# Sample rows of a down product from whole fp32 operands in two column tiles, and another order of projection groups

## The reference, cut to what matters

```python
# input projection: one product, its columns split into seven groups
z = _rms_norm(x, g_attn) @ w_in                      # (tokens, 1024) @ (1024, 2840)
qa, zc, zs, zw, gl, qb, zb = jnp.split(z, ...)       # q, k parts: RMS norm per head, gain, rotary
...
# channel mixer behind the attention, width 2816
h = _rms_norm(x, g_ffn)
a = h @ w_gate
c = conv_b + sum(conv_w[k] * ext[:, k:k + S] for k in range(3))   # ext: earlier rows, then a
y = x + (jax.nn.silu(c) * (h @ w_up)) @ w_down
```

## Time and profile before

| | |
|---|---|
| median of 3 runs | 2040.55 us (2034.24 to 2045.2) |
| profiled execution | 2043.56 us, of it the span 2041.8 us |
| mean granted TensorE clock | 0.976 |
| busy: PE, DVE, ACT, POOL | 92%, 54%, 40%, 13% of the span |
| projection, first to last product | 39.5 to 336.1 us |
| compression and attention | 340 us to about 1064 us |
| output projection and channel mixer | about 1064 us to the end |

### The profile page before, as it was taken

How to read it: one execution, slowest core, us unless ns; L and a number is a source line. 1 busy time by engine, 2 the same in 40 slices (tenths; PEclk the granted TensorE clock), 3 DMA queues, 4 the chain that set the end, 5 groups by cost and what they waited for, 6 DMA issues and landing times. The chain is left out here.

```text
span 2041.8 us, 30807 instructions
## 1 busy us (share of the span) xinstructions
PE 1884.3 (92%) x11675; PEld 1548.7 (76%) x11675; DVE 1108.5 (54%) x2625; ACT 820.3 (40%) x1739; POOL 273.1 (13%) x347
## 2 busy tenths in 40 slices
PE   5997999989998888888869999999999999999998
PEld 4776776877887777777757878888888887887886
DVE  5866872337776677777754434444444444444444
ACT  4444441117777666666643232212212212212211
POOL 1000000004444344444320000000000000000000
PEclk8998999989999999999989999999999999999999
DMA  5333233415665222222335223023023023024002
GB/s 178 111 115 120 88 114 102 138 41 154 175 169 145 84 88 86 85 87 82 104 90 174 62 62 104 25 79 103 26 78 103 28 76 104 29 75 144 31 11 92
DMA packets 171945, 192.12 MB, mean 94 GB/s; under 512 B 55302, under 2 KB 138502, under 8 KB 169528
## 3 DMA queue, kind: packets, MB, share of 16 engines
q1 hardware_dynamic: 169458, 175.56, 27.6%
q0 software_dynamic: 2352, 14.73, 2.2%
HBM read 168.72 MB, written 59.81 MB: 112 GB/s over the span
## 5 line engine op out<-in xcount | busy, mean ns | idle before, releaser
L1838 DVE CUSTOM_DVE_ANT_0 l_e<-l_s,k_masks 128x1024 f32<-128x1024 f32 (+3 forms) x192 | 138.2, 720 | 78.8 <-PE l_s L1483 77.3
L2265 PE MATMUL o_py<-f_h_hi,m_gu_hi 128*128 128x512 f32 x704 | 179.7, 397 | 0.0
L2265 PE MATMUL o_py<-f_h_lo,m_gu_hi 128*128 128x512 f32 x704 | 178.4, 395 | 0.0
L2265 PE MATMUL o_py<-f_h_hi,m_gu_lo 128*128 128x512 f32 x704 | 178.4, 395 | 0.0
L1737 ACT ACTIVATE l_pT_hi<-l_t 128x512 fp32r<-128x512 f32 (+3 forms) x288 | 125.5, 471 | 124.2 <-PE l_t L1523 122.7
L1780 ACT ACTIVATE l_e<-l_e,l_nmin 128x640 f32<-128x640 f32 (+11 forms) x224 | 169.6, 757 | 12.3 <-DVE l_nmin L1838 10.1
L1908 DVE TENSOR_TENSOR l_pT_lo<-l_t,l_pT_hi 128x512 fp32r<-128x512 f32 (+3 forms) x288 | 143.2, 525 | 27.5 <-ACT l_pT_hi L1737 26.8
L2265 PEld LDWEIGHTS o_py<-f_h_lo,m_gu_hi 128*128 128x128 f32 x704 | 131.9, 187 | 32.3
L2265 PEld LDWEIGHTS o_py<-f_h_hi,m_gu_lo 128*128 128x128 f32 x704 | 131.9, 187 | 32.3
L2523 DVE SCALAR_TENSOR_TENSOR a_kv_nat<-m_ext,m_taps,a_kv_nat 128x512 f32<-128x512 f32 x22 | 16.6, 753 | 249.9 <-ACT m_ext L2414 249.9
L2265 PEld LDWEIGHTS o_py<-f_h_hi,m_gu_hi 128*128 128x128 f32 x704 | 129.6, 188 | 29.8
(11 more groups left out here) (320 smaller groups left out, 3975.4 us busy)
## 6 DMA issues: line engine op xcount, KB each, us to landing
m_raw_gu<-in_w_gate SPq DMA_DIRECT2D x22, 512.0 KB, 5.2
m_raw_gu<-in_w_up SPq DMA_DIRECT2D x22, 512.0 KB, 6.3
m_raw_d<-in_w_down SPq DMA_DIRECT2D x11, 1024.0 KB, 5.0
k_first<-in_w_in SPq DMA_DIRECT2D x5, 2048.0 KB, 8.0
a_kd_k<-in_state_dil SPq DMA_DIRECT2D x8, 1024.0 KB
a_kd_v<-in_state_dil SPq DMA_DIRECT2D x8, 1024.0 KB
a_kd_k<-in_cache_slc SPq DMA_DIRECT2D x128, 64.0 KB, 1.8
k_w<-in_w POOLq DMA_DIRECT2D x4, 1024.0 KB, 5.5
```

Of the source, the lines that this page charges most:

```text
L1838: return nc.vector.tensor_tensor_reduce(out=dst, in0=src, in1=m, scale=1.0, scalar=CLAMP, op0=ALU.add, op1=ALU.min, accum_out=low)
L2265: last = nc.tensor.matmul(bank[q % 3][:, 0:w], ws[k][:, m, c, :], hs[:, c, t0:t0 + w], start=(j == 0 and c == 0), stop=(j == 2 and c == KC ...
```

## The change

The list of groups puts win_gate last. Since everything in `project` is written by position in that list, nothing else of that function changes: banks, z buffers, loads and waits follow the new order, POOL's constants and gathers keep their counts of tiles.

In the mixer the sample rows' two down units become one. Its operands are not split: the gated product of the sample parts goes straight into `g_s` (fp32), and the weights are the raw ones. For each of the two chunks two products are made, one for each half of the output columns, into partitions 0 to 63 and 64 to 127 of one bank: two column tiles of TensorE. So 4 products of whole fp32 stand in place of 12 of split operands. The sample tile of x is kept in the same form (half the columns moved to partitions 64 to 127 by a DMA at the start), so one add of 128x512 does for it, and y_sample is stored in two pieces. The sample parts' splits on ScalarE and VectorE go. The raw w_down is read by the unit, so the next load waits for the unit rather than for the split. In the last pair the split of part 3 is moved up, from the body of part 4 to the end of that of part 3.

```diff
 GROUPS = [
     ("qa", 0, 512, (2, 4), (0, 1)),
     ("cmp_slc", 512, 512, (2, 2), (1, 3)),
-    ("win_gate", 1024, 280, (1, 2), (3, 4)),
     ("qb", 1304, 512, (2, 4), (4, 5)),
     ("kb", 1816, 512, (2, 4), (5, 6)),
     ("vb", 2328, 512, None, None),
+    ("win_gate", 1024, 280, (1, 2), (3, 4)),
 ]
...
-        UNITS_D = 2 * STEPS
+        UNITS_D = 2 * TILES + 1
+        PROMPT_PARTS = (0, 1, 3, 4)
...
-        DOWN = [*range(0, 8), 16, 17, *range(8, 16)]
-        DOWN_AFTER = {0: range(0, 10), 2: range(10, 18)}
+        DOWN = [*range(0, 8), 16, *range(8, 16)]
+        DOWN_AFTER = {0: range(0, 9), 2: range(9, 17)}
+
+        def down_bank(i, d):
+            return pd[(i * UNITS_D + d) % 3]
...
             load_gu(0, 0)
-
+            sp.wait_ge(y_added, STEPS)
+            sp.dma_start(x[NS:P, TILES, 0:HALF], x[0:NS, TILES, HALF:D]).then_inc(x_moved, 16)
             sp.wait_ge(y_filled, STEPS)
             load_wd(0)
...
+                if i > 0:
+                    sp.wait_ge(d_filled, (i - 1) * UNITS_D + DOWN.index(2 * TILES) + 1)
+                    load_wd(i)
...
-                    sp.wait_ge(wd_lo_done, i + 1)
-                    load_wd(i + 1)
...
                     if d == 0:
                         pe.wait_ge(wd_lo_done, i + 1)
-                    if d in (0, 8, 10):
-
-                        pe.wait_ge(g_lo_done, i * NP + {0: 4, 8: 6, 10: 5}[d])
+                    if d == 8:
+                        pe.wait_ge(g_made, i * NP + NP)
+                    if d in (0, 9):
+
+                        pe.wait_ge(g_lo_done, i * 4 + {0: 3, 9: 4}[d])
 
                     pe.wait_ge(d_added, i * UNITS_D + (d + 1))
-                    for n in range(6):
-                        k, j = n // 3, n % 3
-                        a, w = ((g_hi, wd_hi), (g_hi, wd_lo), (g_lo, wd_hi))[j]
-                        last = nc.tensor.matmul(pd[d % 3][0:r, :], a[:, k, tok], w[:, k, hs], start=(n == 0), stop=(n == 5))
+                    if tile == TILES:
+                        for k in range(2):
+                            for x in range(2):
+                                last = nc.tensor.matmul(down_bank(i, d)[x * NS:(x + 1) * NS, :], g_s[:, k, :], raw_d[:, k, x * HALF:(x + 1) * HALF],
+                                                        start=(k == 0), stop=(k == 1))
+                    else:
+                        for n in range(6):
...
# ScalarE, body of a pair (VectorE follows it)
                     if q == 0:
-                        if not first:
-                            split_g(i - 1, NP - 1)
...
-                        split_g(i, q - 1)
+                        if q != 3 and not (last and q == 4):
+                            split_g(i, q - 1)
...
                     if q == (3 if last else 4):
                         act.wait_ge(wd_in, i * 16 + 16)
                         nc.scalar.activation(wd_hi[:], raw_d, ACT.Copy).then_inc(wd_hi_done, 1)
+                    if last and q == 3:
+                        split_g(i, 3)
...
-                    nc.vector.tensor_tensor(gated[q % 2][:, 0:w], c, u, ALU.mult).then_inc(g_made, 1)
+                    nc.vector.tensor_tensor(gated[q % 2][:, 0:w] if q % 3 < 2 else g_s[:, k, :], c, u, ALU.mult).then_inc(g_made, 1)
```

More of the change, by code:

```diff
@@ L2054, in finish @@
         gated = [sb("m_gated", [P, 512])[:], hn[:, 1, 512:D]]
-        g_hi = sb("m_g_hi", [P, 2, TOK], F32R)
+        g_hi = sb("m_g_hi", [P, 2, SEQ], F32R)
         rows_s = sb("m_rows_s", [NS, 2 * P])
@@ L2059, in finish @@
         ext = sb("m_ext", [P, CONV_W - 1 + SEQ])
-        g_lo = sb("m_g_lo", [P, 2, TOK], F32R)
+        g_lo = sb("m_g_lo", [P, 2, SEQ], F32R)
+        g_s = sb("m_g_s", [P, 2, NS])
         ph = ps("o_ph", [P, D])
@@ L2083, in finish @@
                                     "s_filled s_copied passed").split())
+        x_moved = sem("m_x_moved")
         gu_in = [sem(f"m_gu_in{m}") for m in range(2)]
-        UNITS_D = 2 * STEPS
+        UNITS_D = 2 * TILES + 1
+        PROMPT_PARTS = (0, 1, 3, 4)
         NP = 6
@@ L2182, in _ @@
             for n in range(STEPS):
-                sp.wait_ge(d_added, 3 + (PAIRS - 1) * UNITS_D + DOWN.index(2 * n + 1) + 1)
+                sp.wait_ge(d_added, 3 + (PAIRS - 1) * UNITS_D + DOWN.index(2 * n + (n < TILES)) + 1)
                 if n < TILES:
@@ L2187, in _ @@
                 else:
-                    sp.dma_start(o["y_sample"].rearrange("b s d -> (b s) d"), x[0:NS, n, :]).then_inc(y_out, 16)
+                    for half in range(2):
+                        sp.dma_start(o["y_sample"].rearrange("b s d -> (b s) d")[:, half * HALF:(half + 1) * HALF],
+                                     x[half * NS:(half + 1) * NS, n, 0:HALF]).then_inc(y_out, 16)
             sp.wait_ge(kept_rows, 6)
@@ L2192, in _ @@
                 sp.dma_start(o["conv_sample"].rearrange("b w f -> (b w) f")[:, cols], src[CONV_W - 1:KEPT]).then_inc(y_out, 16)
-            sp.wait_ge(y_out, 16 * (STEPS + 4))
+            sp.wait_ge(y_out, 16 * (STEPS + 5))
             sp.wait_ge(past_out, 16 * (PIECES + 2))
@@ L2290, in down @@
                     tile, half = DOWN[d] // 2, DOWN[d] % 2
-                    r = P if tile < TILES else NS
-                    tok, hs = slice(tile * P, tile * P + r), slice(half * HALF, (half + 1) * HALF)
                     if d == 0:
                         pe.wait_ge(wd_lo_done, i + 1)
-                    if d in (0, 8, 10):
-                        pe.wait_ge(g_lo_done, i * NP + {0: 4, 8: 6, 10: 5}[d])
+                    if d == 8:
+                        pe.wait_ge(g_made, i * NP + NP)
+                    if d in (0, 9):
+                        pe.wait_ge(g_lo_done, i * 4 + {0: 3, 9: 4}[d])
                     pe.wait_ge(d_added, i * UNITS_D + (d + 1))
-                    for n in range(6):
-                        k, j = n // 3, n % 3
-                        a, w = ((g_hi, wd_hi), (g_hi, wd_lo), (g_lo, wd_hi))[j]
-                        last = nc.tensor.matmul(pd[d % 3][0:r, :], a[:, k, tok], w[:, k, hs], start=(n == 0), stop=(n == 5))
+                    if tile == TILES:
[5 more added lines that the diff above has]
+                        for n in range(6):
+                            k, j = n // 3, n % 3
+                            a, w = ((g_hi, wd_hi), (g_hi, wd_lo), (g_lo, wd_hi))[j]
+                            last = nc.tensor.matmul(down_bank(i, d), a[:, k, tile * P:(tile + 1) * P], w[:, k, half * HALF:(half + 1) * HALF],
+                                                    start=(n == 0), stop=(n == 5))
                     last.then_inc(d_filled, 1)
@@ L2441, in body @@
                         nc.scalar.activation(wd_hi[:], raw_d, ACT.Copy).then_inc(wd_hi_done, 1)
+                    if last and q == 3:
+                        split_g(i, 3)
             loop_pairs(act, body)
-            split_g(PAIRS - 1, NP - 1)
         @block.vector
@@ L2500, in split_g @@
                 k, (t0, w) = q // 3, PARTS[q % 3]
-                dve.wait_ge(g_hi_done, i * NP + (q + 1))
+                dve.wait_ge(g_hi_done, i * 4 + PROMPT_PARTS.index(q) + 1)
                 nc.vector.tensor_tensor(g_lo[:, k, t0:t0 + w], gated[q % 2][:, 0:w], g_hi[:, k, t0:t0 + w].bitcast(F32), ALU.subtract).then_inc(g_lo_done, 1)
@@ L2506, in add @@
                     tile, half = DOWN[d] // 2, DOWN[d] % 2
-                    r = P if tile < TILES else NS
-                    xs = x[0:r, tile, half * HALF:(half + 1) * HALF]
+                    xs = x[:, tile, half * HALF:(half + 1) * HALF]
+                    if i == 0 and tile == TILES:
+                        dve.wait_ge(x_moved, 16)
                     dve.wait_ge(d_filled, i * UNITS_D + (d + 1))
-                    nc.vector.tensor_tensor(xs, pd[d % 3][0:r, :], xs, ALU.add).then_inc(d_added, 1)
+                    nc.vector.tensor_tensor(xs, down_bank(i, d), xs, ALU.add).then_inc(d_added, 1)
             def body(i, first, last):
@@ L2526, in body @@
                     if not first:
-                        add(i - 1, {0: range(0, 2), 1: range(10, 11), 2: range(12, 13)}.get(q, ()))
+                        add(i - 1, {0: range(0, 2), 1: range(9, 10), 2: range(11, 12)}.get(q, ()))
                     dve.wait_ge(silu_done, i * NP + (q + 1))
-                    nc.vector.tensor_tensor(gated[q % 2][:, 0:w], c, u, ALU.mult).then_inc(g_made, 1)
-                    if not first and q == 0:
-                        split_g(i - 1, NP - 1)
+                    nc.vector.tensor_tensor(gated[q % 2][:, 0:w] if q % 3 < 2 else g_s[:, k, :], c, u, ALU.mult).then_inc(g_made, 1)
                     if not first:
-                        add(i - 1, {0: range(2, 10), 1: range(11, 12), 2: range(13, 18)}.get(q, ()))
-                    if q > 0:
+                        add(i - 1, {0: range(2, 9), 1: range(10, 11), 2: range(12, 17)}.get(q, ()))
+                    if q in (1, 2, 5) or q == 4 and not last:
                         split_g(i, q - 1)
```

## The result

The changed kernel takes **2019.85 us** (median of 4 runs, 2018.61 to 2021.59); the kernel before, run beside it, 2041.62 (2034.24 to 2045.2). The ratio is 0.9904, 95% interval 0.9879 to 0.993. The profiled execution took 2020.92 us, its span is 2019.1 us.

The account below looks back on a forecast made before the run. TensorE's products bound mixing and projection, except the 280-column group, where 18.3 us are lost. Terms 9.5 + 8.5 + 3.7 = 21.7 us less gave 2021.9 profiled, 2018.9 as median; 2020 was predicted, range 2010 to 2034.

Parts of the forecast that it names:

- Projection, 9.5 less: Projection's group order: the stretch from the end of cmp_slc to the next stage falls from 202.5 us, 9.5 less.
- kb's: Projection, kb group: 52.2 us as now plus 1.7 for a constant load near the weights' load, 53.9; bounds 52.2 and 56.7.
- POOL's gathers follow the tile counts ... and nothing waits: Projection's last group: the last gather is issued at its fourth tile, some 25 us ahead of the next stage, delaying nothing.
- the upper bound of 0.7 less: Projection: with all groups at their upper bounds the new stretch is still 0.7 us shorter than before.
- Sample unit, 8.5 less: Mixer, sample rows' down product: unit of 1.9 us in place of 2.75, saving 0.85 in each of ten pairs.
- a rival with two waits of 0.16: Mixer's sample unit: each tiling mode change drains TensorE for 0.16 us, unit 2.1, ten save 6.5; no chance given.
- Tail, 3.7 less: Mixer's tail: a 2.5 us stall replaces the 4.70 one, 3.7 us less, bounds 2.9 and 4.6.
- 1.7 to be lost again: Mixer's tail: if the clock falls behind the new stall as behind the old, 1.7 of the 4.6 us gain is lost.
- Tiles in series: Rival, sample unit: 64-column tiles run one after another, 1.8 us more per unit, 11 times; 2040, no change; chance 0.08.
- The stall of 9.66: Rival, projection: the stall moves into qb or kb, 12.4 with the slow tile, less 2 counted; 2030.5; chance 0.11.
- Slower by the clock: Rival, mixer: each sample unit leaves TensorE at 1.2 GHz, 3.6 us more 11 times, 40; 2060; chance 0.06.
- Nothing lost in the tail, loads hidden: Rival, projection and tail: loads hidden, no wait in the last group, nothing lost in the tail; 30 less, 2011; chance 0.12.

Follow-up runs that it names:

- experiment 2: Changed kernel with win_gate (the 280 columns) put back as third group, so sample unit and tail alone: 2028.76 us, 0.9934 of before.
- experiment 7: Changed kernel with two 1 MB constant loads, next to the third and fourth groups' weights' loads, moved two token tiles later: 2020.24 us, 0.9904 of before.
- experiment 9: Changed kernel with POOL's last two gathers of cached pages issued earlier: 2020.1 us, 0.9891 of before.
- experiment 3: Changed kernel with the sample rows' product as two units of one 64-column tile each, instead of two tiles side by side: 2040.37 us, 0.9994 of before.
- experiment 4: Changed kernel with the sample unit's two loops exchanged, both products of the left column tile first: 2021.32 us, 0.9903 of before.
- experiment 10: Changed kernel with three edits together, tail adds early, two constant loads later and last two gathers earlier: 2012.03 us, 0.9858 of before.
- 6: Changed kernel with the tail's first three adds ahead of VectorE's last two splits in the last pair: 2016.37 us, 0.988 of before.
- 8: Changed kernel with the tail's first three adds early and the two constant loads later: 2015.54 us, 0.9876 of before.

## Why the prediction was right, step by step

2020 was forecast, 2019.85 measured. The three terms, their sizes taken from the stretches:

**Projection, 9.5 less.** Measured 8.4 by the changed kernel's profile against the first of before (8.6 on the span's clock), 8.9 by the means of three profiles of before (303.0) and six with this order and these loads (294.1); experiment 2 has the old order too, and with its 301.0 among those of before it is 8.4. The forecast lengths were 51.4, 53.9 and 49.3 us for qb, kb and vb; 51.9, 53.8 and 49.0 came. kb's was right for the reason given, a constant load beside the weights' (experiment 7). Two steps were too short. cmp_slc took 50.3 where 49.3 stood (49.2 as before, and 0.1): the load of 2 MB behind it made ScalarE wait and TensorE stand 0.8 us. And the 280 columns took 32.2 to the last product where 30.0 stood. The step that failed there is "POOL's gathers follow the tile counts ... and nothing waits": the last gather held up a gate store, and by the turn of the z buffers TensorE (experiment 9, where the group takes 30.5 without it). Most of these 2.2 us came back behind the last product, where 6.2 us passed to the next stage in place of 8.0: it began 38.4 us into the group, 38.0 forecast. One sum is off beside this: the upper bound of 0.7 less counts some 53.8 for qb, 4.5 on the clean 49.3; with 4.5 on the 51.4, as the list reads, the stretch would be 1.5 longer than before.

**Sample unit, 8.5 less.** Ten pairs became 7.1 us shorter, 0.71 each instead of 0.85. That tiles run side by side was right (experiments 3 and 4); the cost around them was mis-sized. In the rows after, the unit starts 0.33 behind the last prompt product, whose pace is 0.23: 0.10. It takes 1.87 to the next product. The first eight products behind it take 0.99, which the second eight do in 0.93. Together 2.03 in place of 1.9. The one-tile kernel has the same 0.33 ahead of its unit, and its second unit follows the first in the same tile after 1.76, and that is what the earlier trace rows show for two such products; so this is not a price of having two tiles. Nor is it one of changing from 128 to 64 columns alone: before, the split sample units have 64 columns too, and there the first starts 0.23 behind the last prompt product, the next part 0.23 behind the last of them, and its first eight take 0.94:
```profile
1412.88 0.39 PE L2303 MATMUL o_ph<-m_wd_hi,m_g_lo 128*128 128x512 f32 x1
...
1415.63 0.39 PE L2303 MATMUL o_ph<-m_wd_hi,m_g_lo 128*64 128x512 f32 x1
...
1416.80 1.09 PE L2277 MATMUL o_py<-m_gu_hi,f_h_lo 128*64 128x256 f32 x8
```
The price came with the products of whole fp32 operands. The prediction weighed a rival with two waits of 0.16, at 2.1 for the unit. It is the rule of the Trainium skill, TensorEngine Tiling (Array Packing), Key Properties, that a change of tiling mode drains TensorE. The measured 2.03 lies nearer to 2.1 than to the 1.9 that stood in the sum, and the saving of 0.71 nearer to 0.65 than to 0.85. By its size that rival deserved more weight than the narrower tiles of the earlier trace rows; whether a drain is the reason, no run here shows.

**Tail, 3.7 less.** A stall of 2.5 us was forecast behind the third unit: 2.31 came, ahead of the fourth, for the reason named, an add queued behind VectorE's last split. From the last turn to the end of the down units the first profile of before takes 31.8 us, the changed kernel 29.0: 2.8. The two later profiles of before take 33.0, because some 14 of their products in place of 8 run at low clock behind the 4.70, and against them it is 4.0. The size therefore hangs on the clock, as the bound said: 1.7 to be lost again, and eight starts 0.40 to 0.43 apart instead of 0.23 are 1.5.

The three measured terms make 18.3 to 20.0 where 21.7 stood; that the span shrank by 22.7 is the longer second stretch of the first profile. The medians differ by 21.8, and the interval of the ratio (14 to 25 us) covers both. So the mechanisms were right in the main, but that 2020 was met to 0.2 us is luck: 1.8 to 3.5 us of the 21.8 lie in none of the three terms, about as much as the first two were forecast too large.

**The rivals.** Tiles in series would have made the unit 3.7: experiment 3 has its products in series, 3.57, and the kernel gains nothing. The stall of 9.66 did not move as a whole; its largest remainder is 2.71. Slower by the clock did not occur: the granted clock is 1.00 from 1400 to 1600 us. "Nothing lost in the tail, loads hidden", priced at 2011, was not what the change did, but experiment 10 comes near it: 2012, with a stall of 1.1 us left in kb.

## What to carry to other kernels

Where a pipeline's stages differ in length, look at what each one hides for the next: a short stage in the middle exposes a load that a long one would cover, and at the end it has none to cover. But other queues that count steps rather than stages (here POOL's constants and gathers) then meet other neighbours; look up where each of their transfers lands in the new order. Behind the last stage of a pipeline, an in-order engine's remaining work should be put in the order in which it is needed, as the three adds show: 4 us for no work saved.

## What the runs showed of the hardware

- Two column tiles of 64 with 512 columns of whole fp32 each run fully side by side (1.87 us for eight records against 1.76 for four), in either order of writing.
- Products of whole fp32 in 64 columns cost 0.10 us on the way in from split products, and some 0.15 on the way out: the next product starts 0.52 behind the last record, where records start 0.42 apart, and its first eight take 0.99 in place of 0.93. It is so with one tile and with two. Split products of 64 columns at the same place lose nothing on either way (0.23 from start to start, before).
- The clock behind a short pause is not certain. Behind the same stall of 2.31 us at the same place the granted clock fell to 0.50, 1.2 GHz, in five kernels (after, experiments 2, 3, 4 and 7) and stayed at 1.00, 2.4 GHz, in one (experiment 9), each profiled once; without the stall it did not fall (6, 8, 10).
